# A two-block network on one core: the memory projection moved into the front stage, and attention rebuilt with weights normalised in their transposition

## The reference, cut to what matters

```python
def neighborhood_attention(q, k, v, rpb):
    ...
        scores = jnp.einsum('bwhd,biwjhd->bhwij', q_r, k_win).astype(jnp.float32) + bias.astype(jnp.float32)[None]
        probs = jax.nn.softmax(scores.reshape(b, h, GRID_W, kr * kc), axis=-1).reshape(b, h, GRID_W, kr, kc)
        return jnp.einsum('bhwij,biwjhd->bwhd', probs.astype(v.dtype), v_win)

def memory_attention(q, mem_h, w_mem_kv):
    mk, mv = jnp.split(mem_h @ w_mem_kv, 2, axis=-1)
    ...
    scores = jnp.einsum('bshd,bmhd->bhsm', qh, kh).astype(jnp.float32)
    probs = jax.nn.softmax(scores, axis=-1)
    return jnp.einsum('bhsm,bmhd->bshd', probs.astype(vh.dtype), vh).reshape(b, s, MEM_WIDTH)

# second_block
        h = rms_norm(x, norm_mix_g[l])
        (na_q, na_k, na_v, ..., mem_q, gate_na, gate_rw, gate_mem) = split_columns(h @ w_in[l])
        y_na = neighborhood_attention(...)
        y_rw = rwkv7_bidirectional(...)
        y_mem = memory_attention(mem_q, rms_norm(mem, norm_mem_g[l]), w_mem_kv[l])
```

## Time and profile before

| what | us |
|---|---|
| median of 3 runs | 3317.74 (3312.02 to 3319.58) |
| profiled execution, whole time | 3313.01 |
| its span | 3310.9 |
| PE busy | 2830.3 (85%) |
| DVE busy | 1266.3 (38%) |
| ACT busy | 789.4 (24%) |
| weight tile of the front, 512 KB, issue to landing | 3.4 |

### The profile page before, as it was taken

The page is one execution under the profiler, slowest core; times in us unless marked ns, Lnnn a source line. Parts: engine busy times, 40 slices in busy tenths (PEclk is TensorE's granted clock), DMA queues, the critical chain, the costliest instruction groups (busy, mean ns, idle before and its releaser), DMA issues. The chain is left out here.

```text
span 3310.9 us, 45205 instructions
## 1 busy us (share of the span) xinstructions
PE 2830.3 (85%) x18878; PEld 2035.8 (61%) x18878; DVE 1266.3 (38%) x2093; ACT 789.4 (24%) x1247; POOL 110.5 (3%) x90
## 2 busy tenths in 40 slices
PE   8999867699799698999598998667888888888887
PEld 7999745499799697777477886554323323233222
DVE  5664655443455533664243335523111111111112
ACT  3212154432333322441232332411000000000001
POOL 0000012000000000000002221000000000000000
PEclk9999977799899899999758999887999999899998
DMA  4336430344433453333300000656999999999994
GB/s 137 135 127 162 87 124 11 114 152 127 124 111 112 126 147 100 129 116 133 144 16 15 1 2 7 194 178 250 405 411 389 392 405 399 399 391 393 417 410 200
DMA packets 225397, 636.79 MB, mean 192 GB/s; under 512 B 39808, under 2 KB 137088, under 8 KB 200192
## 3 DMA queue, kind: packets, MB, share of 16 engines
q1 hardware_dynamic: 190096, 577.45, 46.6%
q10 hardware_dynamic: 35120, 56.74, 4.9%
HBM read 581.86 MB, written 49.92 MB: 191 GB/s over the span
## 5 line engine op out<-in xcount | busy, mean ns | idle before, releaser
L3293 PE MATMUL moe_bank<-moe_ring,moe_z 128*64 128x512 f32 x2048 | 525.1, 660 | 134.1 <-DMA moe_ring<-in_w_exp_up 133.3
L3293 PEld LDWEIGHTS moe_bank<-moe_ring,moe_z 128*64 128x64 f32 x2048 | 161.2, 150 | 439.1 <-issue 431.5
L3493 DVE TENSOR_TENSOR moe_sg<-moe_sg,moe_bank 64x512 f32<-64x512 f32 x64 | 44.1, 690 | 658.6 <-ACT moe_sg L3396 658.6
L64 PE MATMUL in_bank<-in_x_low,in_w_high 128*128 128x264 f32 x896 | 259.3, 289 | 6.1 <-DVE in_w_low L1194 6.0
L66 PE MATMUL in_bank<-in_x_high,in_w_high 128*128 128x264 f32 x896 | 255.6, 285 | 0.0
L65 PE MATMUL in_bank<-in_x_high,in_w_low 128*128 128x264 f32 x896 | 255.5, 285 | 0.0
L64 PE MATMUL merge_y<-merge_x_low,merge_w_high 128*128 128x264 f32 (+1 forms) x640 | 203.9, 319 | 56.4 <-DVE merge_w_low L533 50.4
L3321 PE MATMUL moe_bank<-moe_ring,moe_act_t 128*64 128x512 f32 x1024 | 230.6, 592 | 0.5 <-ACT moe_act_t L3403 0.5
L64 PE MATMUL up_prod<-up_x_low,up_w_high 128*128 128x264 f32 x704 | 201.7, 287 | 0.0
L66 PE MATMUL up_prod<-up_x_high,up_w_high 128*128 128x264 f32 x704 | 200.8, 285 | 0.0
L65 PE MATMUL merge_y<-merge_x_high,merge_w_low 128*128 128x264 f32 (+1 forms) x640 | 200.4, 313 | 0.0
(11 more groups left out here) (496 smaller groups left out, 5342.4 us busy)
## 6 DMA issues: line engine op xcount, KB each, us to landing
moe_ring<-in_w_exp_gate SPq DMA_DIRECT2D x64, 2048.0 KB, 13.5
moe_ring<-in_w_exp_up SPq DMA_DIRECT2D x64, 2048.0 KB, 17.9
moe_ring<-in_w_exp_down SPq DMA_DIRECT2D x64, 2048.0 KB, 9.0
in_w<-in_w_in SPq DMA_DIRECT2D x56, 512.0 KB, 3.4
front_w<-in_w_in SPq DMA_DIRECT2D x46, 512.0 KB, 3.4
up_w<-in_w_up SPq DMA_DIRECT2D x44, 512.0 KB, 5.0
p<-in_out ACTq DMA_DIRECT2D x48, 264.0 KB, 2.0
down_w<-in_w_down SPq DMA_DIRECT2D x8, 1408.0 KB, 9.0
```

The source lines that it names most:

```text
L64: nc.tensor.matmul(to, w_high, x_low, start=start, stop=False)
L3293: last = nc.tensor.matmul(bank[64 * g:64 * g + 64, s], xe[:, (e // BATCH) % 2, k, at:at + CAPACITY], ring[:, (3 * n + g) % RING, k * HALF: ...
L3493: nc.vector.tensor_tensor(sg[0:CAPACITY, s], sg[0:CAPACITY, s], bank[64:64 + CAPACITY, s], ALU.mult).then_inc(act_ready, 1)
```

## The change

Three things change.

The stage `mem_kv` is gone. Its weights are four more tiles of 128 columns behind the front's 46 (n = 46 to 49 of 50), and they are multiplied with the memory, 256 columns wide. The memory is loaded by SP ahead of weight tile 34, once `bonus_ready` has reached 2, into room that the preparation has left; its high and low parts, squares, sum and scale are made on ACT, DVE and PE while tiles 35 to 40 are worked on. The store of a tile is now issued by ACT one tile later, behind the next cast.

In attention the exponentials also give their row sums (`accum_out`), DVE makes `weights`, the identity scaled by the reciprocals, and `turn` is now a matmul with the exponentials as the stationary operand and `weights` as the moving one. `values` has the value columns (64) as the stationary operand and the turned weights (128) as the moving one, with the two heads of a pair on the two halves of the output partitions, so that the output is already by channels. The 20 transpositions and five copies at the end are gone. Three units of scores run ahead instead of two, over four buffers.

In `rwkv7`, PE waits only for the identity, DVE for the masks, and the other four constants are waited for later.

```diff
 NA_FIRST = (0, 8, 24, 32)
+RING = 4
+AHEAD = 3
...
@@ -1981,12 +1982,13 @@
                 for c in range(CT["na"]):
                     sp.dma_start(bias[:, 2 * c:2 * c + 2], bias_dram[:, 2 * c:2 * c + 2]).then_inc(bias_loaded[c], 16)
                     if c == 0:
+                        sp.wait_ge(qk_loaded, 32)
                         sp.dma_start(v["mem"][:], mem_kv_dram[MEM_WIDTH:].rearrange("(c p) t -> p c t", p=P)).then_inc(
                             mem_v_loaded, 16)
...
                 def turn(n):
-                    pe.wait_ge(p_ready, 2 * (n + 1))
+                    pe.wait_ge(weights_ready, 2 * (n + 1))
                     if n >= 2:
                         pe.wait_ge(p_turn_ready, n - 1)
                     for e in range(2):
                         for j in range(2):
-                            last = nc.tensor.transpose(bank[:, 4 + n % 2, (2 * e + j) * P:(2 * e + j + 1) * P],
-                                                       s[:, n % 3, e, j * P:(j + 1) * P], ident[:])
+                            last = nc.tensor.matmul(bank[:, 4 + n % 2, (2 * e + j) * P:(2 * e + j + 1) * P],
+                                                    s[:, n % RING, e, j * P:(j + 1) * P], weights[:, n % 2, e], start=True, stop=True)
                     last.then_inc(p_turn_made, 1)
 
                 def values(n):
...
-                    for e in range(2):
-                        for j, tile in enumerate(v_tiles_of(n)):
-                            last = nc.tensor.matmul(bank[:, 6 + n % 2, e * SIDE:(e + 1) * SIDE], p_turned[:, n % 2, e, j],
-                                                    v_tok[:, tile, 2 * c + e], start=(j == 0), stop=(j == 1))
+                    for j, tile in enumerate(v_tiles_of(n)):
+                        for e in range(2):
+                            head = slice((2 * c + e) * HEAD_DIM, (2 * c + e + 1) * HEAD_DIM)
+                            last = nc.tensor.matmul(bank[64 * e:64 * e + 64, 6 + n % 2, 0:P], v_tok[:, tile, head],
+                                                    p_turned[:, n % 2, e, j], start=(j == 0), stop=(j == 1))
                     last.then_inc(y_made, 1)
 
                 pe.wait_ge(ident_loaded, 16)
                 pe.wait_ge(qk_loaded, 32)
-                scores(0)
-                scores(1)
-                for j in range(len(v_tiles)):
-                    if j == 2 * QT:
-                        pe.wait_ge(mem_v_loaded, 16)
-                    turn_values(j)
+                for n in range(AHEAD):
+                    if n == 2:
+                        for j in range(len(v_tiles)):
+                            if j == 2 * QT:
+                                pe.wait_ge(mem_v_loaded, 16)
+                            turn_values(j)
+                    scores(n)
                 pe.wait_ge(v_turn_ready, len(v_tiles))
-                pe.wait_ge(ones_ready, 1)
                 turn(0)
                 for n in range(U):
-                    if n + 2 < U:
-                        scores(n + 2)
+                    if n + AHEAD < U:
+                        scores(n + AHEAD)
                     if n + 1 < U:
                         turn(n + 1)
                     values(n)
-                for o, (kind, c) in enumerate(outs):
-                    pe.wait_ge(y_ready, U)
-                    if o >= 2:
-                        pe.wait_ge(out_ready, o - 1)
-                    for t in range(QT):
-                        last = nc.tensor.transpose(bank[:, o % 2, t * P:(t + 1) * P], y_tok[kind][:, t, c * P:(c + 1) * P], ident[:])
-                    last.then_inc(out_turned, 1)
...
+                def weigh(n):
+                    dve.wait_ge(p_ready, 2 * (n + 1))
+                    nc.vector.reciprocal(inverse[:, n], total[:, n]).then_inc(inverse_ready, 1)
+                    dve.wait_ge(inverse_ready, n + 1)
+                    if n == 0:
+                        dve.wait_ge(ident_loaded, 16)
+                    if n >= 2:
+                        dve.wait_ge(p_turn_made, n - 1)
+                    for e in range(2):
+                        nc.vector.tensor_scalar(weights[:, n % 2, e], ident[:], inverse[:, n, e:e + 1], None, ALU.mult).then_inc(
+                            weights_ready, 1)
 
                 def finish(n):
                     kind, c, t = pairs[n]
                     dve.wait_ge(y_made, n + 1)
-                    made = bank[:, 6 + n % 2, 0:2 * SIDE].rearrange("p (e m) -> p e m", e=2)
-                    nc.vector.reciprocal(inverse[:, n], made[:, :, HEAD_DIM]).then_inc(inverse_ready, 1)
-                    dve.wait_ge(inverse_ready, n + 1)
-                    nc.vector.tensor_tensor(y_tok[kind][:, t, c * P:(c + 1) * P].rearrange("p (e m) -> p e m", e=2),
-                                            made[:, :, 0:HEAD_DIM], inverse[:, n].unsqueeze(2).broadcast_to([P, 2, HEAD_DIM]),
-                                            ALU.mult).then_inc(y_ready, 1)
-
-                soften(0)
-                soften(1)
+                    made = bank[:, 6 + n % 2, 0:P]
+                    if kind == "na":
+                        nc.vector.tensor_copy(grid(y[kind], c, slice(0, GRID_ROWS), t * BLOCK_W, BLOCK_W),
+                                              made.rearrange("p (r w) -> p r w", r=GRID_ROWS)).then_inc(y_ready, 1)
+                    else:
+                        nc.vector.tensor_copy(y[kind][:, c, t * P:(t + 1) * P], made).then_inc(y_ready, 1)
+
+                for n in range(AHEAD):
+                    soften(n)
+                    if n >= 1:
+                        weigh(n - 1)
                 for n in range(U):
+                    if n + AHEAD < U:
+                        soften(n + AHEAD)
                     if n + 2 < U:
-                        soften(n + 2)
+                        weigh(n + 2)
                     finish(n)
...
                 def exponentials(n):
                     act.wait_ge(low_ready, n + 1)
                     for e in range(2):
-                        nc.scalar.activation(s[:, n % 3, e], s[:, n % 3, e], ACT.Exp, bias=low[:, n, e:e + 1]).then_inc(p_ready, 1)
-
-                exponentials(0)
-                for n in range(U):
-                    if n + 1 < U:
-                        exponentials(n + 1)
+                        nc.scalar.activation(s[:, n % RING, e], s[:, n % RING, e], ACT.Exp, bias=low[:, n, e:e + 1],
+                                             accum_out=total[:, n, e:e + 1]).then_inc(p_ready, 1)
+
+                def turned(n):
                     act.wait_ge(p_turn_made, n + 1)
                     if n >= 2:
                         act.wait_ge(y_made, n - 1)
                     nc.scalar.copy(p_turned[:, n % 2].rearrange("p e j m -> p (e j m)"), bank[:, 4 + n % 2]).then_inc(
                         p_turn_ready, 1)
-                for o, (kind, c) in enumerate(outs):
...
-                        nc.scalar.copy(y[kind][:, c], bank[:, o % 2]).then_inc(out_ready, 1)
+
+                exponentials(0)
+                exponentials(1)
+                turned(0)
+                for n in range(U):
+                    if n + 2 < U:
+                        exponentials(n + 2)
+                    if n + 1 < U:
+                        turned(n + 1)
...
+                    if n == FRONT_MEM:
+                        sp.wait_ge(bonus_ready, 2)
+                        sp.dma_start(mem, mem_dram.rearrange("(k p) t -> p k t", p=P)).then_inc(mem_loaded, 16)
+                        sp.dma_start(mem_gain[:], mem_gain_dram).then_inc(mem_loaded, 16)
...
+                    if n >= FRONT_TILES:
+                        pe.wait_ge(mem_low_ready, KT)
+                        for k in range(KT):
+                            done = three_passes(nc, bank[:, n % 4, 0:TM], w_high[:, s, k], w_low[:, s, k],
+                                                mem_high[:, k], mem_low[:, k], k == 0, k == KT - 1)
+                        done.then_inc(y_ready, 1)
+                        return
...
+                def memory(i):
+                    if i == 2:
+                        act.wait_ge(consts_ready, 6)
+                    if i in (2, 3):
+                        act.wait_ge(mem_loaded, 32)
+                        act.wait_ge(bonus_ready, 2)
+                        for k in range(4 * (i - 2), 4 * (i - 2) + 4):
+                            nc.scalar.activation(mem_high[:, k], mem[:, k], ACT.Copy,
+                                                 scale=mem_gain[:, k:k + 1]).then_inc(mem_high_ready, 1)
...
+                    if i == 7:
+                        act.wait_ge(mem_sum_made, 1)
+                        nc.scalar.activation(mem_scale[:], bank[:, 7, 0:TM], ACT.Ln, bias=eps[:, 0:1], scale=1.0 / K).then_inc(
+                            mem_scale_ready, 1)
+                        act.wait_ge(mem_scale_ready, 1)
+                        nc.scalar.activation(mem_scale[:], mem_scale[:], ACT.Exp, scale=-0.5).then_inc(mem_scale_ready, 1)
```

(22 more changed lines are left out.)

128 lines of the change are left out of this document (87 added, 41 removed).

## The result

The changed kernel takes 3228.4 us (median of 4 executions, 3224.84 to 3234.97) against 3318.2 (4, 3312.02 to 3319.58): a ratio of 0.9735, 95% interval 0.9715 to 0.9756. Forecast were 3257, with a range of 3244 to 3283.

The account below looks back on a forecast made before the run. PE at half clock was taken to bound attention, at 3.80 us a unit. Gains of 26.5 (front), 29 (attention) and 2.5 (`rwkv7`) summed to 58, taking 3313.0 to 3255, stated as 3257 us; range 3244 to 3283.

Parts of the forecast that it names:

- Part 1: Front: working the memory's projection as four more tiles there removes the `mem_kv` stage, gaining 26.5 us.
- 39.0 - 11.5 - 0.6 - 0.4: Front: `mem_kv` removed, less four added tiles, PE's sum of squares and an allowance for narrow margins: 26.5 us.
- wrong if the clock is, and by little otherwise: Closing sign: the forecast fails if attention's granted clock isn't near 1.00, and otherwise misses only slightly.
- Rivals 4 and 5: Front: stall for memory's load or low part, 3263 us, 5%; late tile 34 weights halve PE's clock, 3344 us, 2%.
- Part 2: Attention: the rebuilt unit holds full clock, with DVE the bound at 2.48 us a unit; gain 29 us.
- The restart at half clock: Attention: 3 us added for PE restarting at half clock after the pause, moving the stage's end to 1706.
- My estimates of streaming: Attention: data streams 68% of an old unit, 86% of a new one at half clock, 70% at full clock.
- Part 3: Start of `rwkv7`: PE waits for the identity alone, gaining 2.5 us, bounds 0 and 3.
- The clock's going up and down: Rival for attention: half the units at 4.06 us and half at 2.48, 13.4 us more, 3270 us; chance 22%.
- Rival 2: Attention: clock stays at half, so only about 2 of the 29 us are gained, 3282 to 3286 us; chance 12%.
- Rival 3: Attention: pairs of `values` don't run side by side; 3261 us at full clock, 3299 at half; chance 4%.

Follow-up runs that it names:

- the repetition: The changed kernel itself measured again, nothing altered, beside three other variants: 3228.9 us.
- the pause filled: The kernel before, with 11 unused 128x128 identity products on PE in the pause before attention's first turn: 3284.1 us, ratio 0.9908.
- the POOL kernel: The changed kernel with normalisation moved to POOL, scaling the exponentials in place, and `turn` as plain transpositions: 3240.3 us, ratio to before 0.9776.
- the run with plain transpositions: The changed kernel with `turn` as four plain transpositions, weights left unnormalised, for timing only: 3234.0 us.
- the heads apart: The changed kernel with the loops of `values` exchanged, both key tiles of head 0 before those of head 1: 3229.6 us, ratio to before 0.9739.
- fillers: The changed kernel with unused PE products, 40 at attention's start, 8 at its end, 8 at `rwkv7`'s start: 3226.0 us, ratio to before 0.9731.
- POOL as well: The changed kernel with both the filler products and the normalisation on POOL with plain transpositions: 3240.4 us, ratio to before 0.9768.

## Why the prediction was right and wrong

**The sum, Part 1: the missing term.** Folding the memory in was put at 26.5. The stage gained 42.4, of which the store gives 16.0 by the run that puts it back, and 26.4 remain. That this meets the 26.5 to 0.1 is luck, since the stage varies by 3 to 4 us from profile to profile. The rows of the tiles say it better: 39.0 - 11.5 - 0.9 = 26.6. The step that failed is the sum "39.0 - 11.5 - 0.6 - 0.4", which takes the plain tiles of the front as they were: the later store, told in the change, has no term in it. Two runs show the term, 16.0 us undone and 11 to 14 alone. With 16 the forecast would have been 3241, and the 13 us that it still lacks are attention's 4.6, the 6 of `rwkv7`, and the spread of the stages left alone. The prediction ends on "wrong if the clock is, and by little otherwise": the clock came out as chosen, and the forecast was wrong by 29 us all the same. Rivals 4 and 5 priced a stall for the memory's load; it came to 0.23 us of PE.

**Part 2, the size.** 29 were forecast, 33.6 measured. DVE was named the bound with 2.48 a unit; it needs 2.09, since the 0.04 that I put between instructions isn't lost: DVE's rows overlap by up to 0.1 (two scalings take 0.48 busy, and 0.39 until the next). PE was put at 2.15 and takes 2.31. So the wrong engine, and 0.17 x 17 = 2.9 us of the 4.6. The two scalings at 0.24 each were within the bounds. The restart at half clock, put at 3 us, was there, 0.65 in the first window of the units, and cost about 1: where the clock fell behind that pause attention took 71.7 and 71.8 us, where it didn't 70.6 and 70.7 (the repetition, and the store put back). That is most of the rest.

```profile
1608.00:1612.00 4.00, 2.96 (x12) 2.14 (x12) 2.49 (x8) 2.18 (x10) 0.00 (x0) 0.65 0.01 3
```

**Part 2, the mechanism: half right.** The clock was said to stand or fall by the form of the unit. That the old form can't hold 1.00 is refuted: with the pause filled it held it to the end, with PE only 36.35 of 40 us busy. What let it fall was the pause of 2.77 us before the first turn. A pause lets it fall, but not each time: after one of 1.6 us it fell in two of six profiles of the changed kernel and its variants. What the form decides is whether it comes back: the old unit stayed at 0.50 for 65 us, while the rebuilt one, the old one with products in `turn` and the POOL kernel's, with transpositions and the new values, had 1.00 again 3.5 to 5.2 us after PE's restart. My estimates of streaming (68% old; 3.46 of 4.06, 85% rather than the 86 printed, new at half clock) point that way; which quantity the chip goes by isn't shown.

Of the Trainium skill's rule ("TensorE: Matmul & The Clock Gate", Part 4, transpositions don't count as busy) the runs leave this. For it: products in `turn` bring the clock back. Against it: with POOL the unit's transpositions stayed and the clock came back too. And in the run with plain transpositions nothing else ran on PE from 1609.2, and the clock rose among them; two us of `scores` had run just ahead, so this alone would not settle it.

```profile
1609.20:1609.70 0.50, 0.50 (x4) 0.48 (x3) 0.50 (x1) 0.00 (x0) 0.00 (x0) 0.50 0.99 410
...
1612.20:1612.70 0.50, 0.50 (x4) 0.28 (x3) 0.00 (x0) 0.43 (x1) 0.00 (x0) 1.00 0.89 377
```

A product streams twice as many records as a transposition, so the two explanations of the run with products aren't told apart by it. The Trainium skill's rule on tiling modes ("TensorEngine Tiling (Array Packing)", Key Properties) leaves room for the 2.31: by an estimate from the earlier trace rows the three groups stream 0.43 + 0.86 + 0.44 = 1.73 at full clock, and the three changes of mode could hold the other 0.58; no run removed one, so that is not shown.

**Part 3.** 2.5 were forecast; the first product came 3.3 us sooner, just above the upper bound of 3. The stage gained 8.7 because the clock also rose sooner, for which the sum had no term. When it rises for good varies between kernels whose code in this stage is the same: 12 us behind the first transfer in the changed kernel and in its repetition (stages of 326.1 and 325.6), 21 with the store put back (331.0), 19 with the heads apart (328.2). With the old start it is 20 to 25 (330.4 to 334.8), so the stage's length goes with the rise. The two levels, one behind the other, with the store put back:

```profile
1690.00:1697.00 7.00, 6.33 (x28) 5.88 (x28) 0.84 (x2) 1.15 (x2) 0.00 (x0) 0.50 0.00 0
1698.00:1704.00 6.00, 5.62 (x44) 4.54 (x44) 2.88 (x7) 1.32 (x3) 2.45 (x2) 0.95 0.01 3
```

So up to 5 us of this term hang on something outside the stage's own code. Whether they change from one execution of a kernel to the next isn't shown, since each profile is a single one. What decides it stays open; with fillers it was 12 us, and 11 with POOL as well, where POOL alone had 20.

**Rivals.** The clock's going up and down (22%) and its staying at half (12%) didn't come about. Rival 2's "about 2 of the 29" is 29 - 26.8 - 4.5 + 3 = 0.7 by its own terms. Rival 3 is out by the 0.58 us of `values`. No rival ended below the forecast by more than 7 us: the range was closed downwards at 3244 by the bounds of terms that I had, and the missing term lay outside it.

## What to carry to other kernels

When a diff moves a wait on an in-order queue, list what stood behind it and look for that chain where its engines are fullest, not in the quiet tiles: the releaser printed beside the cast named it. When PE shows 100% busy at a clock of 0.50, look for the pause in which it fell before rebuilding the work; eleven products of no use bought 28.5 us of a stage whose rebuilding gained 33.6. And a forecast's lower end should leave room for an edit that got no price.

## What the runs showed of the hardware

- The old attention unit holds either level of the clock for its whole stage: 0.50 in before's profile, 1.00 with the pause filled, 2.33 or 3.80 us a unit. Two of ten executions of the kernel with the store moved had the higher mean clock and were 30 us faster without any change to attention.
- After a fall the clock came back in 3.5 to 5.2 us in the rebuilt unit, in the old one with products in `turn`, and in the POOL kernel's unit with plain transpositions; in the old unit it did not come back in 65.
- Eight float32 records with 64 stationary and 128 moving columns, for two heads that write different halves of the output partitions, take 0.58 us, and 0.59 when the program gives one head after the other.
- POOL takes 0.9 us to scale 128x256 in SBUF, where DVE scales 128x128 in 0.24.
